# Two hybrid blocks on one core: where VectorE and ScalarE wait for their own results

## The reference

```
h    = rms_norm(x) * (1 + scale) + shift          # scale, shift, gate = silu(c) @ w_ada + b_ada
proj = h @ w_in                                   # 2048 -> 6144: u, z_s, q, k, v, z_a
y_s  = s5_mixer(u) * silu(z_s)                    # complex diagonal state space over the 256 tokens, gelu, w_glu
y_a  = diff_attention(rope(q), rope(k), v) * silu(z_a)   # 8 heads, difference of two softmaxes
x    = x + gate * (concat(y_s, y_a) @ w_out)
```

## Time and profile before

| | |
|---|---|
| median of 3 timed runs | 3186.14 us (3178.17 to 3191.81) |
| profiled execution: span (the page gives no other time for it) | 3189.6 us |
| TensorE busy | 2961.5 us, 93% |
| VectorE busy | 2245.6 us, 70%, 3501 instructions |
| ScalarE busy | 1610.2 us, 50%, 2404 instructions |
| GpSimd busy | 285.1 us, 9% |
| mean granted TensorE clock | 0.964 |
| moved by DMA | 580.99 MB, mean 182 GB/s |

### The profile page before, as it was taken

The page is one execution under the profiler, slowest core; times in us unless marked ns, Lnnn a source line. Parts: engine busy times, 40 slices in busy tenths (PEclk is TensorE's granted clock), DMA queues, the critical chain, the costliest instruction groups (busy, mean ns, idle before and its releaser), DMA issues.

```text
span 3189.6 us, 60331 instructions
## 1 busy us (share of the span) xinstructions
PE 2961.5 (93%) x24208; PEld 2735.8 (86%) x24208; DVE 2245.6 (70%) x3501; ACT 1610.2 (50%) x2404; POOL 285.1 (9%) x488
## 2 busy tenths in 40 slices
PE   6899998998988889999899999999899999999987
PEld 2577777787978789999888889989899999999987
DVE  6367777687788887776566666666688846887565
ACT  3345555365555555745334342545555544555554
POOL 0011211100112220300000001010000000000000
PEclk8899999998999999999999999999899999999999
DMA  9887676874645456454233333555455555555543
GB/s 371 303 262 246 234 244 227 283 277 155 176 139 160 136 156 213 164 186 160 97 106 111 103 112 108 164 167 184 132 176 186 180 196 179 183 183 171 187 150 120
DMA packets 168232, 580.99 MB, mean 182 GB/s; under 512 B 40272, under 2 KB 40304, under 8 KB 155536
## 3 DMA queue, kind: packets, MB, share of 16 engines
q1 hardware_dynamic: 146784, 525.40, 50.0%
q0 software_dynamic: 20592, 48.26, 4.9%
q10 hardware_dynamic: 576, 3.47, 0.3%
HBM read 555.22 MB, written 21.76 MB: 181 GB/s over the span
## 4 chain that ended last, share of the span: by engine, by line
PE 59%; DVE 22%; ACT 8%; DMA 7%; issue 3%; SPq 1%; POOL 0%; DVEq 0%; ACTq 0%
PE acc L977 58%; DVE arena L937 6%; DVE rounded L937 5%; ACT arena L974 4%; ACT rounded L974 3%; DVE upper L937 3%; DVE arena L947 2%; DMA arena<-in_w_in 1%; DMA arena<-in_w_ada 1%; DVE upper L947 1%; DMA arena<-scr_k 1%; DMA scr_k<-arena 1%; ACT upper L974 1%; ACT L974 1%; SPq L933 1%
## 5 line engine op out<-in xcount | busy, mean ns | idle before, releaser
L977 PE MATMUL acc<-rounded 128*128 128x256 f32 x14688 | 1930.9, 290 | 39.2 <-issue 14.3
L977 PEld LDWEIGHTS acc<-rounded 128*128 128x128 f32 x14688 | 1836.6, 195 | 124.2 <-issue 87.9
L937 DVE TENSOR_TENSOR rounded<-arena,rounded 128x1024 fp32r<-128x1024 f32 (+1 forms) x832 | 1004.4, 1207 | 305.1 <-ACT rounded L974 236.4
L974 ACT ACTIVATE rounded<-arena 128x1024 fp32r<-128x1024 f32 (+1 forms) x864 | 884.0, 1023 | 651.3 <-PE acc L977 430.3
L977 PEld LDWEIGHTS acc<-upper_rounded,rounded 128*128 128x128 f32 x4560 | 554.9, 194 | 23.0 <-issue 13.8
L977 PE MATMUL acc<-upper_rounded,rounded 128*128 128x256 f32 x4560 | 562.0, 285 | 7.0 <-DVE rounded L937 3.1
L974 ACT ACTIVATE arena<-arena 128x256 f32<-128x256 f32 (+4 forms) x477 | 253.1, 531 | 298.5 <-DVE arena L937 199.6
L937 DVE TENSOR_TENSOR arena<-arena 128x256 f32<-128x256 f32 (+5 forms) x458 | 244.6, 534 | 51.0 <-ACT arena L974 32.1
L977 PE MATMUL acc<-arena 128*32 128x512 f32 (+8 forms) x1550 | 217.6, 493 | 54.0 <-DVE arena L937 21.7
L947 DVE SCALAR_TENSOR_TENSOR arena<-arena 128x256 f32<-128x256 f32 (+6 forms) x465 | 209.0, 449 | 59.0 <-ACT arena L974 31.3
L937 DVE TENSOR_TENSOR arena<-acc,arena 128x256 f32<-128x256 f32 (+4 forms) x270 | 117.5, 435 | 166.6 <-PE acc L977 143.8
(11 more groups left out here) (92 smaller groups left out, 1194.1 us busy)
## 6 DMA issues: line engine op xcount, KB each, us to landing
arena<-in_w_in SPq DMA_DIRECT2D x328, 512.0 KB, 4.7
arena<-in_w_ada SPq DMA_DIRECT2D x88, 1024.0 KB, 5.6
arena<-in_w_up SPq DMA_DIRECT2D x176, 512.0 KB, 4.2
arena<-in_w_down SPq DMA_DIRECT2D x88, 512.0 KB, 4.1
arena<-in_w_outa SPq DMA_DIRECT2D x32, 512.0 KB, 6.3
arena<-in_w_glu SPq DMA_DIRECT2D x32, 512.0 KB, 6.1
arena<-in_w_outm SPq DMA_DIRECT2D x32, 512.0 KB, 4.7
arena<-in_w_out SPq DMA_DIRECT2D x32, 512.0 KB, 4.4
```

Of the source, the lines that this page charges most:

```text
L937: return self.put(self.e and self.e.tensor_tensor(o, a, b, op))
L974: return self.put(self.e and self.e.activation(o, a, f, scale=scale, **kw))
L977: return self.put(self.e and self.e.matmul(o, l, r, start=start, stop=stop, skip_group_check=True))
```

## The change

`Port.begin` goes, and with it the wait in front of every operation of VectorE and ScalarE. In its place are two calls that the programs make where an operation reads or overwrites what the same engine has just written or is still reading: `settled()` waits for the newest operation of the engine, `after(op)` for a given earlier one. An operation waited for by `after` gets a named increment of its own (`att_top`, `rw_aa`, `rw_kk`, `rw_dd`, `rw_carry`, `s5_vt`, `scaled`). In three places a wait is added that `begin` had covered: `part` for "ya" waits for mla's `y`, `sum4` for the sum before it, and `add_square` for the square sum before it. The order of the operations, their shapes and the work of the other engines are as before. Cut to its core:

```diff
@@ class Op, class Port
-        p.newest, self.told = (sem, p.n[sem]), True
+        self.at, self.told = (sem, p.n[sem]), True
...
-    def begin(self):
-        if self.in_order and self.op is not None:
-            if not self.op.told:
-                self.op.then_inc(self.name + "_step")
-            if self.e is not None:
-                self.wait_value(*self.newest)
+    def settled(self):
+
+        if not self.op.told:
+            self.op.then_inc(self.name + "_step")
+        self.after(self.op)
+
+    def after(self, op):
+
+        if self.e is not None:
+            self.wait_value(*op.at)
...
     def tt(self, o, a, b, op):
-        self.begin()
         return self.put(self.e and self.e.tensor_tensor(o, a, b, op))
@@ scalar_program, part
+        elif tag == "ya":
+            act.wait_ge("mla_act", ("y", j))
@@ scalar_program, s5_sine
         act.act(both(ARE + 128), both(ARE + 256), ACT.Sin, scale=con("nsgn"))
+        act.settled()
         act.act(both(ARE + 256), both(ARE + 256), ACT.Sin, scale=con("sgn")).then_inc("s5_act", ("ph", l, p))
@@ vector_program, turned (turns_of and bounded alike)
+        dve.settled()
         dve.stt(o, k, -c1, th, MUL, ADD)
+        dve.settled()
         dve.stt(o, k, -c2, o, MUL, ADD)
+        dve.settled()
         return dve.stt(o, k, -c3, o, MUL, ADD)
@@ s5_prep
+            vt[0].then_inc("s5_vt")
         if i == 2:
-            dve.tt(V(VV, 512), V(VV, 512), V(TM, 512), ADD).then_inc("s5_dve", ("vv", l, b))
+            dve.after(vt[0])
+            vt[0] = dve.tt(V(VV, 512), V(VV, 512), V(TM, 512), ADD).then_inc("s5_dve", ("vv", l, b))
...
         if i == 3:
+            dve.after(vt[0])
             dve.tt(V(TM, 4, 9, 16), pw(P2, 9), ch(BC + 192, 9), MUL)
+            dve.settled()
             dve.tt(V(CC, 576), V(CC, 576), V(TM, 576), ADD).then_inc("s5_dve", ("cc", l, b))
@@ rw, s == 3
-            dve.stt(V(Af, 256), V(KK, 256), -1.0, V(LD, 256), MUL, MUL)
+            x = dve.stt(V(Af, 256), V(KK, 256), -1.0, V(LD, 256), MUL, MUL).then_inc("rw_kk")
             dve.tt(V(Kf, 256), V(Kf, 256), V(RT2, 256), MUL)
+            dve.after(x)
             dve.tt(V(KK, 256), V(KK, 256), V(AA, 256), MUL)
+            dve.settled()
             dve.tt(V(Bf, 256), V(KK, 256), V(RT2, 256), MUL).then_inc("rw_dve", ("z", i))
@@ sum4, add_square
+        if g > 1:
+            dve.wait_ge("sum_dve", ("hf", g - 1))
...
+        if not first:
+            dve.after(summed[0])
```

More of the change, by code:

```diff
@@ L1852, in scalar_program @@
             play[beat](*of)
-    act.begin()
+    act.settled()
 def rw_place(n):
@@ L1963, in gp @@
         scale = MODC + 48 * l + 16 + 4 * i
+        if l == 0:
+            dve.settled()
         dve.stt(V(GP + 4 * i, 4), V(scale, 4), 1.0, V(PAR + PCOL["norm_g"] + 16 * l + 4 * i, 4), ADD, MUL)
@@ L1969, in h @@
         last = 4 * (k // 4) + 3 if l == 0 else 15
+        if k == 0 or k % 4 == 0 and l == 0:
+            dve.settled()
         for j in ([k] if k % 4 == 0 and l == 0 or k == 0 else []) + ([k + 1] if k < last else []):
@@ L1989, in fin @@
         x = V(X + 256 * k, 256)
+        if k == 0:
+            dve.settled()
         dve.stt(x, x, V(PAR + PCOL["final_g"] + k, 1), V(RS, 256), MUL, MUL).then_inc("x_dve", ("fin", k))
@@ L2062, in s5_setup @@
             dve.memset(V(SN, 128), 0.0).then_inc("s5_dve", ("set", l))
+    vt = [None]
     def s5_prep(l, b, i):
@@ L2175, in kkn @@
         dve.ts(V(KNR, 32), V(KNR, 32), 1e-12, None, MAX)
+        dve.settled()
         dve.recip(V(KNR, 32), V(KNR, 32)).then_inc("rw_dve", "kr")
+    half = [None]
     def rw(i, s, slot):
@@ L2185, in rw @@
             dve.ts(V(LD, 256), V(LD, 256), -0.5 * EXPMH, -0.5 * EXPMH, MUL, ADD)
+            dve.settled()
             dve.scan(V(CU, 256), con("scm"), V(LD, 256))
-            dve.ts(V(AA, 256), V(AA, 256), 0.5, 0.5, MUL, ADD)
+            half[0] = dve.ts(V(AA, 256), V(AA, 256), 0.5, 0.5, MUL, ADD).then_inc("rw_aa")
             t = tile_ready(dve, slot)
@@ L2193, in rw @@
             dve.stt(V(KK, 256), V(Kf, 256), par("k_k", i), B(6, 0, 256), MUL, MUL)
+            dve.after(half[0])
             dve.ts(V(RT2, 256), V(AA, 256), par("k_a", i), V(OKA + i, 1), MUL, ADD)
+            dve.settled()
             dve.tt(V(Kf, 256), V(Kf, 256), V(RT2, 256), MUL)
+            dve.settled()
             dve.stt(V(D2, 256), V(Rf, 256), par("r_k", i), V(Kf, 256), MUL, MUL).then_inc("rw_dve", ("rk", i))
@@ L2337, in ev @@
             dve.wait_ge("mm", ("out", t.o))
+            if (t.name, n) in (("w_in2", 0), ("w_up", 0)):
+                dve.settled()
             dve.tt(V(at, 256, np_=np_), B(b, 0, 256, np_=np_), V(RS if t.name == "w_up" else RSH, 256, np_=np_),
@@ L2450, in vector_program @@
             play[beat](*of)
-    dve.begin()
+    dve.settled()
 def gpsimd_program(pool, m, tl, D):
```

78 lines of the change are left out of this document (60 added, 18 removed).

## The result

The changed kernel takes 3049.19 us (median of 4 runs, 3043.74 to 3055.81) against 3185.33 us before (4 runs, 3178.17 to 3191.81): a ratio of 0.9563, 95% interval 0.9545 to 0.9581, or 136 us less. The profiled execution took 3052.15 us, its span is 3050.3; the profile before has a span of 3189.6, so the two profiles differ by 139 us.

What follows compares the result with a forecast made beforehand. TensorE's matmuls were taken to stand behind VectorE and ScalarE for a third of the time. Stage gains of 50, 13, 23 and 17 us sum to 103, taking 3189.6 to 3086.6 us, stated as 3085, range 3015 to 3150.

Steps and rivals of the forecast that it cites:

- What bounds the kernel: Whole kernel: TensorE has only 59% of the chain of waits, VectorE 22%, ScalarE 8%; nothing to gain from 2330 to 3100 us.
- 600 to 1200: Stretch in us: 80 us of removed waits against 140 us of room, TensorE next, about 60% arrives: 50 us.
- What an own wait costs: VectorE and ScalarE: a removed wait gives 0.12 us alone, 0.19 to 0.20 beside a second, 0 behind a late engine.
- The rival built on the rule: VectorE doesn't overlap because its pipeline empties anyway: 53 us gained, 3133 us; chance 0.20.
- What of it is on the path: Removed waits on the chain: 127 us for VectorE and 59 for ScalarE, together 186 us if all counted.
- nearly all arrives: Rival: stages are chains through one engine, so about 175 of the 186 us are gained: 3011 us; chance 0.08.
- The sum by stages: Gains of 50 (600 to 1200 us), 13 (114 to 600), 23 (1500 to 2120) and 17 (the rest): 103 us.
- 114 to 600: Stretch in us: VectorE 10 and ScalarE 16 us; transfers and their issue are next, so half arrives: 13 us.
- The slower rival: Earlier weight fetches crowd the S5 tap transfers, 140 us lost against 103 gained: 3223 us; chance 0.03.
- one sign of being wrong: S5 tap transfers: the prediction would be wrong if they land later than before; no size given.
- The waits weren't the limit: Rival: the stall moves to partners such as TensorE, only some 10 us gained: 3176 us; chance 0.07.
- What would show it: New trace: VectorE overlaps, dependents keep 0.03 us, DVEq L916 steps mostly go, VectorE's chain share nears 17%, ScalarE's 7%.

Runs made afterwards that it cites:

- lag: Changed kernel plus, before every operation of VectorE and ScalarE, a wait for the operation two back on the same engine: 3056.51 us, ratio 0.9587.
- incs: Changed kernel plus a semaphore increment on every operation of VectorE and ScalarE, with no added wait: 3052.38 us, ratio 0.9576.
- stage: Changed kernel with the own wait kept only in the beats that the kernel before plays from 600 to 1200 us: 3108.50 us, ratio 0.9756.
- swap: Changed kernel with the own wait back before every VectorE and ScalarE operation, written ahead of its other waits: 3167.66 us, ratio 0.9944.

## Why the prediction was right, point by point

**What bounds the kernel** held. The gain came where the chain was VectorE's and ScalarE's, half of it between 600 and 1200 us, and 3 us came from the 770 us that were 95.9% TensorE's. One reading was off: VectorE's visible rows of 600 to 1200 in the earlier trace rows add up to 41.4%, not 44; the 290 us that the sum went on with include the small rows that the view cuts off.

**What an own wait costs** held, and closely: an overlap of 0.08 us on VectorE where I took 0.09 from ScalarE's one row, 0.08 to 0.10 on ScalarE, and 0.03 left at kept waits. The range from nothing to 0.15 was needed, since no VectorE row could show it. In the explanation one thing was too simple: I wrote that the separate wait instruction makes the 0.11. lag has the instruction and no gap; it is issued late only because what it waits for is late.

**The Trainium skill's rule** ("VectorE: DVE Perf Modes", section "The DRAIN you can't avoid"), that chaining operations without semaphores doesn't skip the pipeline's flush, is contradicted here: VectorE's next operation starts 0.03 to 0.11 us behind the end with the wait, 0.08 ahead of it without, and 64% of the gain comes from VectorE alone. The section's own measurement, that a semaphore after each operation costs nothing extra, agrees as far as increments go (incs, 3052 against 3049 us); it is the wait that costs. The section also says that an operation that isn't held starts earlier, and refers to "Two Vector instructions with no wait between them" on the same page; that agrees with the traces. The rival built on the rule, 3133, falls.

**What of it is on the path**: 127 us for VectorE and 59 for ScalarE, 68 to 32. Measured one at a time 64% and 27%. The whole was 186, and 136 arrived, 73%; I had forecast 55%. That puts 3049 about as near to the rival *nearly all arrives* (3011) as to the forecast (3085): the mechanism was right, the discount for the next limit was too large.

**The sum by stages** is where the 36 us between 103 and the 139 of the two profiles lie. Two terms were mis-sized: 600 to 1200 gave 68 for the 50 predicted, 114 to 600 gave 25 for 13. 1500 to 2120 gave 25 for 23, and the rest 21 for 17 (2 + 5 + 11 + 3). I discounted the two by 40% and by half, as TensorE or transfers would take over, and left out what a shorter wait does to TensorE's clock. In the earlier trace rows the clock of 600 to 1200 is 0.95: with levels of 1.2 and 2.4 GHz that is 10% of 600 us at the low one, 60 us; afterwards 0.99 is 2% of 532, 11 us. 49 us fewer at half speed give back up to 25 us, as far as matmuls were running in them. For the stretch ahead it is 39 us (0.96 of 486) and 18 us (0.98 of 461), so up to 10. The first bound covers the 18 us that were missing, the second not quite the 12. At the price that the same work showed between incs and the changed kernel (7 us for 24), 49 us fewer are worth some 14 and 21 fewer some 6, an estimate: most of the first gap and half of the second. TensorE's own rows go with it; of 573 to 1105 us in the changed kernel, against the earlier trace rows:

```profile
L973 PE MATMUL acc<-rounded 128*128 128x256 f32 x2304 | 310.9, 290 | 2.1 <-issue 1.8 <-DVE rounded L941 0.3
L973 PE MATMUL acc<-upper_rounded,rounded 128*128 128x256 f32 x1106 | 138.1, 285 | 0.2 <-DVE rounded L941 0.2
```

The streaming matmuls themselves were busy for 449 us where they were for 470 (326.2 + 144.1). stage, with the waits back and the clock at 0.95 again, goes with it too. But the clock was never changed by itself on purpose, and executions differ in other ways too: ahead of 600 us incs took 466 us for the changed kernel's 461, both at 0.98. That the clock carried this part is an estimate, not shown, and what made up the rest of the second gap is open.

**Transfers were not next.** The chain by line of the changed kernel, 112 to 573 us:

```profile
by line: PE acc L973 46.0%; DMA arena<-scr_k 9.7%; DMA scr_k<-arena 7.0%; DMA arena<-in_w_ada 6.6%; SPq L938 4.8%; DMA arena<-in_w_in 4.8%; ACT arena L970 3.1%; issue 2.9%; POOL arena L938 2.3%; PE acc L976 1.9%; ACT rounded L970 1.8%; DVE 
```

The DMA rows and SPq have a third of it, as in the earlier trace rows (32.9% of 461 us is 152, 31.7% of 486 was 154), yet almost the whole potential of 26 us arrived. The transfers on the chain took as long as before and took over nothing: a share of the chain doesn't say that its owner is next when the rest gets shorter.

**The slower rival** fell where it stood: DMA issues of the changed kernel, 112 to 573 us,

```profile
arena<-scr_k POOLq DMA_DIRECT2D x60, 64.0 KB, 6.4
...
scr_k<-arena POOLq DMA_DIRECT2D x15, 120.0 KB, 4.8
```

and 573 to 1105:

```profile
arena<-scr_k POOLq DMA_DIRECT2D x64, 64.0 KB, 2.7
...
scr_k<-arena POOLq DMA_DIRECT2D x16, 120.0 KB, 3.7
```

6.4 and 4.8 us where the earlier trace rows had 6.2 and 4.5; 2.7 and 3.7 where it had 2.7 and 3.5, at DMA shares of 0.81 and 0.63 for 0.76 and 0.56. 0.5 and 0.2 us a round trip, not the 3.3 from which it decided. By the letter, one sign of being wrong came true, as the tap transfers do land later; at 15 x 0.5 + 16 x 0.2 = 11 us even if all were on the chain, it was too small a sign.

**The waits weren't the limit** was the rival that fell most clearly: ScalarE's rounding now waits longer for TensorE than in the earlier trace rows, as that rival said,

```profile
ACT rounded L970 <- PE acc L973: 589.6, 393, 10.7
```

but the stall moved there because the work ahead is done sooner, and TensorE waits less. A released engine that idles at its next partner is no loss when that partner is the one that sets the end.

**What would show it.** The overlaps, the kept 0.03 and the nearly unchanged 770 us came as written, and of the 412 steps DVEq on the chain 17 are left. The stretch after 600 us was to take 550 and takes 532. The chain's shares, 17% and 7% forecast, are 9% and 4%: I subtracted the saving from the shares and forgot that the chain changes its way when TensorE's own order becomes the longest. Of the 573 to 1105 us stretch, its chain by line:

```profile
by line: PE acc L973 47.9%; DVE arena L941 9.8%; DVE rounded L941 6.1%; ACT arena L970 5.1%; issue 4.1%; ACT rounded L970 3.2%; DVE arena L949 2.8%; ACT L970 2.2%; DMA arena<-scr_k 1.8%; DMA scr_k<-arena 1.8%; DVE upper L949 1.6%; DMA arena
```

TensorE 47.9% where it had 24.9%, VectorE's large rows 9.8, 6.1 and 2.8 where they had 16.5, 11.9 and 5.5. Nor did overlapping make the operations themselves longer; the costliest groups of ScalarE and VectorE on the page (mean ns is the last number ahead of the second bar):

```profile
L970 ACT ACTIVATE rounded<-arena 128x1024 fp32r<-128x1024 f32 (+1 forms) x864 | 875.8, 1020 | 805.4 <-PE acc L973 589.6
L941 DVE TENSOR_TENSOR rounded<-arena,rounded 128x1024 fp32r<-128x1024 f32 (+1 forms) x832 | 986.3, 1197 | 267.4 <-ACT rounded L970 266.9
```

1020 and 1197 ns; 1023 and 1207 ns before, as shown above.

## What to carry to other kernels

On VectorE and ScalarE, wait for an own result only where it is read or overwritten, and count what a needless wait costs by the operations on the chain, not by their time: here about 0.12 us alone and 0.19 beside another wait, and three quarters of that sum arrived. Where some own wait must stay, one on an older operation, satisfied while the predecessor still runs, is nearly free; it is the wait for the predecessor that costs. Before discounting a stage's gain for the engine that comes next, see whether anything shows that its time grows when yours shrinks, and look at TensorE's clock in that stage, which here rose from 0.95 to 0.99.

## What the runs showed of the hardware

- VectorE starts an operation without an own wait 0.08 us before the end that the profile gives its predecessor, ScalarE 0.08 to 0.10 us before; with a wait for the predecessor, and no other, 0.03 to 0.04 us behind it.
- Of two waits in front of an operation, the one written last became an instruction of its own, and the operation followed the end of that wait 0.07 to 0.08 us later than it follows a wait that it carries itself (0.11 in place of 0.03 to 0.04). So in this kernel the wait that is expected to end last is better written first: in the kernel before the other engine's wait stood first, in swap the predecessor's.
- A satisfied wait in a separate instruction costs next to nothing: with some 2770 more of them lag took 3056.5 us against 3049.2. An increment on every operation costs nothing that can be told from noise (incs, 3052.4).
- The same 4847 matmuls with the work around them took 596 us at a mean clock of TensorE of 0.97 (the changed kernel) and 589 us at 0.99 (incs).
